# A routed-expert block whose gathers are reordered: tile loops written out, the lead of the down gathers raised from 16 to 24 rows, and gathers issued in turns of four up and four down rows

## The reference, cut to what matters

```python
def peer_block(xb, w_q, sub_keys, expert_u, expert_v):
    T = xb.shape[0]
    q = (xb @ w_q).reshape(T, PEER_HEADS, 2, PEER_HALF)
    s = jnp.einsum('thpd,hpkd->thpk', q, sub_keys)
    sv, si = lax.top_k(s, PEER_TOPK)
    cand = (sv[:, :, 0, :, None] + sv[:, :, 1, None, :]).reshape(T, PEER_HEADS, PEER_TOPK * PEER_TOPK)
    ...
    top_s, pos = lax.top_k(cand, PEER_TOPK)
    eidx = jnp.take_along_axis(cidx, pos, axis=-1)
    gate = jax.nn.softmax(top_s.astype(jnp.float32), axis=-1).astype(xb.dtype)
    u = jnp.take(expert_u, eidx, axis=0)
    act = jax.nn.gelu(jnp.einsum('thkd,td->thk', u, xb))
    v = jnp.take(expert_v, eidx, axis=0)
    return jnp.einsum('thk,thkd->td', gate * act, v)
```

## Time and profile before

| | |
|---|---|
| median of 3 runs | 4076.16 us (4074.84 to 4086.3) |
| profiled execution, its own time | 4073.35 us |
| its span | 4071.4 us |
| gathers of layer one, first to last | 523 to 2184 us |
| gathers of layer two, first to last | 2341 to 4002 us |
| bytes moved by gathers | 1073.87 MB of 1168.56 MB |

### The profile page before, as it was taken

The page is one execution under the profiler, slowest core; times in us unless marked ns, Lnnn a source line. Parts: engine busy times, 40 slices in busy tenths (PEclk is TensorE's granted clock), DMA queues, the critical chain, the costliest instruction groups (busy, mean ns, idle before and its releaser), DMA issues.

```text
span 4071.4 us, 34938 instructions
## 1 busy us (share of the span) xinstructions
PE 2006.1 (49%) x9949; PEld 931.6 (23%) x9949; DVE 2019.2 (50%) x4967; ACT 685.6 (17%) x1897; POOL 2056.6 (51%) x2098
## 2 busy tenths in 40 slices
PE   8998963443433333333437954333333333333447
PEld 3554541111111111111213431111111111111213
DVE  1425265555555555555552255555555555555551
ACT  2112121111111111112111111111111111112112
POOL 1413136565655555555562045555555555555661
PEclk9998886666666666666568976666666666666668
DMA  5312359898988888889997268888888888889992
GB/s 199 124 52 83 134 188 340 324 342 307 345 331 331 323 329 330 327 329 361 335 341 260 83 251 333 330 330 327 333 331 328 323 330 336 325 323 357 341 362 103
DMA packets 334241, 1168.56 MB, mean 287 GB/s; under 512 B 36026, under 2 KB 39380, under 8 KB 331732
## 3 DMA queue, kind: packets, MB, share of 16 engines
q0 software_dynamic: 294912, 1073.87, 70.2%
q1 hardware_dynamic: 39124, 92.27, 6.1%
HBM read 1163.92 MB, written 2.10 MB: 286 GB/s over the span
## 4 chain that ended last, share of the span: by engine, by line
another core or an unknown queue 47%; PE 18%; ACT 10%; issue 8%; DVE 6%; POOL 3%; DMA 3%; POOLq 0%; ACTq 0%; DVEq 0%
PE banks L701 14%; ACT ring L1405 4%; PE banks L1039 4%; DVE scr L1903 2%; ACT L1397 2%; ACT L1385 2%; POOL scr L646 2%; POOL ring L652 2%; DMA ring<-in_peer_up,idx_v 1%; DMA ring<-in_expert_v,idx_v 1%; ACT scr L1385 0%; ACT hT L1223 0%; ACT ring L1375 0%; ACT scr L1397 0%
## 5 line engine op out<-in xcount | busy, mean ns | idle before, releaser
L1039 PE MATMUL banks<-ring 128*32 128x512 f32 x4096 | 874.6, 950 | 1642.2 <-ACT ring L1405 736.6
L1903 DVE CUSTOM_DVE_ANT_0 scr<-scr,banks 128x1024 f32<-128x1024 f32 x1024 | 1207.2, 1218 | 578.7 <-DMA scr<-in_expert_u,idx 271.1
L646 POOL DMA_INDIRECT scr<-in_expert_u,idx x512 | 480.9, 939 | 542.4 <-DVE idx L1882 156.0
L646 POOL DMA_INDIRECT scr<-in_peer_down,idx x512 | 480.7, 939 | 422.9 <-DVE scr L1903 155.8
L1039 PEld LDWEIGHTS banks<-ring 128*32 128x32 f32 x4096 | 177.5, 153 | 2126.3 <-issue 1983.2
L652 POOL DMA_INDIRECT ring<-in_expert_v,idx_v x512 | 480.2, 938 | 312.7 <-issue 145.7
L652 POOL DMA_INDIRECT ring<-in_peer_up,idx_v x512 | 480.6, 939 | 306.5 <-issue 150.2
L701 PE MATMUL banks<-ring,scr 128*128 128x128 f32 (+1 forms) x2112 | 287.4, 297 | 8.6 <-ACT ring L1427 5.2
L701 PEld LDWEIGHTS banks<-ring,scr 128*128 128x128 f32 x2112 | 259.7, 201 | 85.0 <-issue 81.6
L1375 ACT ACTIVATE ring<-banks 128x256 f32<-128x256 f32 x64 | 24.5, 383 | 1457.6 <-remote 1391.4
L701 PE MATMUL banks<-ring,hT 128*128 128x512 f32 x512 | 224.6, 596 | 1.8 <-DVE hT L1808 1.0
(11 more groups left out here) (211 smaller groups left out, 2067.6 us busy)
## 6 DMA issues: line engine op xcount, KB each, us to landing
ring<-in_w_mod SPq DMA_DIRECT2D x12, 2048.0 KB, 8.8
ring<-in_w_in SPq DMA_DIRECT2D x7, 2048.0 KB, 12.9
scr<-in_peer_w_q SPq DMA_DIRECT2D x1, 8192.0 KB
scr<-in_peer_down,idx POOLq DMA_INDIRECT x512
ring<-in_peer_up,idx_v POOLq DMA_INDIRECT x512
scr<-in_w_q SPq DMA_DIRECT2D x1, 8192.0 KB
scr<-in_expert_u,idx POOLq DMA_INDIRECT x512
ring<-in_expert_v,idx_v POOLq DMA_INDIRECT x512
```

The lines of the kernel that those rows point to most:

```text
L646: nc.gpsimd.indirect_dma_start(u_rows[:, k % SLOTS, :], None, table_u, bass.IndirectOffsetOnAxis(idx[:, h % IDX_SLOTS, k:k + 1], 0)).then_ ...
L1039: last = nc.tensor.matmul(psum[2 + c][32 * g:32 * g + 32, :], spread[:, h % 2, k, :], v_rows[k % SLOTS][:, c * CW:(c + 1) * CW], start=(h ...
L1903: V.tensor_tensor_reduce(u_rows[:, k % SLOTS, :], u_rows[:, k % SLOTS, :], xn, 1.0, 0.0, ALU.mult, ALU.add, dots[:, h % 2, k:k + 1]).then_ ...
```

## The change

The tile loops and `hold` go, and all four engines run through `for j in range(32)` written out, with plain waits on constants. On POOL 24 down gathers come first (`U_LEAD`), then four up gathers, four down gathers that are 24 ranks ahead, four up gathers, and so on. On DVE the order becomes: route j + 1, weights j - 1, dot products 0 to 7 of j, softmax j + 1, dot products 8 to 15, pack_idx j + 1; `add_output` moves behind the ninth dot product of the next tile's second head. On PE `scores_q` j + 3 moves ahead of b0 of head j, `scores_s` j + 3 ahead of b1, `block_rows` ahead of b2 of a tile's seventh head, `move_weights` j + 1 ahead of b3 of head j, and `move_idx` j + 3 (instead of n + 2) to the end of head j. On ACT the order becomes gelu j, exponentials j + 2, copy of the weights and spread j, copies of head j + 3. Two gate tiles of the second layer's end get other banks, and TensorE waits there for `w_packed` once more.

```diff
 V_CREDIT = 64
+N_HEADS = TT * PH
+U_LEAD = TOPK + SLOTS
...
-        def move_bank(h, last_tile):
-            return 6 if last_tile and h == PH - 1 else 4 + h % 2
...
-        def hold(eng, s, value):
-            eng.wait_ge(s, value)
-            eng.sem_inc(passed, 1)
...
             def gathers(layer, table_u, table_v, last_projection):
-                def u_gather(n, h, k):
-                    hold(pool, u_used, n * TOPK + (k + 1))
+                n0 = layer * N_HEADS
...
+                def u_gather(j, k):
+                    n = n0 + j
+                    if k == 0:
+                        pool.wait_ge(routed, n + 3)
+                    pool.wait_ge(u_used, n * TOPK + (k + 1))
                     nc.gpsimd.indirect_dma_start(u_rows[:, k % SLOTS, :], None, table_u,
...
-                def v_gather(n, h, k):
-                    hold(pool, v_used, n * TOPK + (k + 1 - SLOTS + V_CREDIT))
+                def v_gather(j, k):
+                    n = n0 + j
+                    if k == 0:
+                        pool.wait_ge(idx_packed, n + 1)
+                    pool.wait_ge(v_used, n * TOPK + (k + 1 - SLOTS + V_CREDIT))
...
-                def token_block(first, more):
-                    for h in range(PH):
-                        u_too = h < PH - 1 or more
-                        hold(pool, idx_packed, first + (h + 1))
-                        if u_too:
-                            hold(pool, routed, first + (h + 4))
...
-                            if u_too:
-                                u_gather(first + (h + 1), (h + 1) % PH, k)
-                            v_gather(first + h, h, k)
-                n0 = layer * TT * PH
-                pool.wait_ge(routed, n0 + 3)
-                for k in range(TOPK):
-                    u_gather(n0, 0, k)
+                for i in range(U_LEAD):
+                    u_gather(i // TOPK, i % TOPK)
                 full(pool, *last_projection)
-                with pool.Fori(0, TT - 1) as b:
-                    token_block(b * PH + n0, True)
-                token_block(n0 + (TT - 1) * PH, False)
+                for first in range(0, N_HEADS * TOPK, QUADS):
+                    for i in range(first, first + QUADS):
+                        v_gather(i // TOPK, i % TOPK)
+                    for i in range(first + U_LEAD, min(first + U_LEAD + QUADS, N_HEADS * TOPK)):
+                        u_gather(i // TOPK, i % TOPK)
...
+                def scores_q(j):
+                    n, h = n0 + j, j % PH
+                    if h == 0 and j > 0:
...
-                    if not first:
+                    if j >= 2:
                         pe.wait_ge(s_copied, n - 1)
                         pe.wait_ge(idx_packed, n - 1)
...
-                def move_idx(n, h):
+                def move_idx(j):
+                    n = n0 + j
                     pe.wait_ge(idx_expanded, n + 1)
-                    to_quads(psum[4 + h % 2], 0, idx_x).then_inc(idx_moved, 1)
...
-                def move_weights(n, h, bank, more):
...
+                def move_weights(j):
+                    n = n0 + j
                     pe.wait_ge(weighted, n + 1)
+                    pe.wait_ge(s_copied, min(n + 3, n0 + N_HEADS))
                     pe.wait_ge(idx_packed, n + 1)
-                    if more:
-                        pe.wait_ge(s_copied, n + 3)
-                    to_quads(psum[bank], 2 * P, weight[:, h % 2, :, :]).then_inc(w_moved, 1)
...
-                def add_up(n, h, scores_too):
+                    to_quads(psum[4 + n % 2], 2 * P, weight[:, n % 2, :, :]).then_inc(w_moved, 1)
+                def add_up(j):
+                    n, h = n0 + j, j % PH
+                    if h == 0:
+                        pe.wait_ge(x_added, n // PH + 1)
+                    if j + 3 < N_HEADS:
+                        scores_q(j + 3)
                     for b in range(TOPK // QUADS):
-                        if b == 2 and scores_too:
-                            scores_q(n + 3, (h + 3) % PH)
-                        if b == 3 and scores_too:
-                            scores_s(n + 3, (h + 3) % PH)
+                        if b == 1 and j + 3 < N_HEADS:
+                            scores_s(j + 3)
+                        if b == 2 and h == PH - 2 and j + 2 < N_HEADS:
+                            pe.wait_ge(u_used, (n + 2) * TOPK + SLOTS)
+                            block_rows()
+                        if b == 3 and j + 1 < N_HEADS:
+                            move_weights(j + 1)
                         pe.wait_ge(spread_set, n * TOPK + QUADS * (b + 1))
...
-                def token_block(it, more, beside={}):
-                    for h in range(PH):
-                        if h == PH - 3 and more:
-                            pe.wait_ge(x_cur_set, it + 2)
-                        if h == 0:
...
-                            pe.wait_ge(u_used, it * (PH * TOPK) + (PH * TOPK + SLOTS))
-                            block_rows()
-                        if not more and h == PH - 1:
-                            all_empty(pe, *last_rows)
-                        move_weights(it * PH + h, h, move_bank(h, not more), h < PH - 2 or more)
-                        add_up(it * PH + h, h, h < PH - 3 or more)
-                        if h < PH - 2 or more:
...
+                    if j + 3 < N_HEADS:
+                        move_idx(j + 3)
...
-                def activations_and_weights(n, h, bank, beside=None):
+                def gelu_of(j):
+                    n = n0 + j
                     act.wait_ge(u_used, n * TOPK + (TOPK + SLOTS))
-                    nc.scalar.activation(gelu[:, h % 2, :], dots[:, h % 2, :], gelu_func).then_inc(gelu_done, 1)
-                    if beside:
-                        beside()
-                    hold(act, w_moved, n + 1)
-                    nc.scalar.activation(packed_w[:, h % 2, :], psum[bank][:, 2 * P:2 * P + TOPK], ACT.Copy).then_inc(w_packed, 1)
+                    nc.scalar.activation(gelu[:, n % 2, :], dots[:, n % 2, :], gelu_func).then_inc(gelu_done, 1)
...
+                def spread_out(j):
+                    n = n0 + j
+                    act.wait_ge(w_moved, n + 1)
+                    nc.scalar.activation(packed_w[:, n % 2, :], psum[4 + n % 2][:, 2 * P:2 * P + TOPK], ACT.Copy).then_inc(w_packed, 1)
                     act.wait_ge(w_packed, n + 1)
                     act.wait_ge(v_used, n * TOPK + (V_CREDIT - TOPK))
                     for k in range(TOPK):
...
-                def token_block(it, b, more, beside={}):
-                    for h in range(1, PH):
-                        head(it * PH + h, h, 3 if more else PH - 1 - h, beside.get(h), not more)
...
-                        head(it * PH + PH, 0)
+                        nc.scalar.activation(spread[:, n % 2, k, :], e32, ACT.Copy,
+                                             scale=packed_w[:, n % 2, col_of(k):col_of(k) + 1]).then_inc(spread_set, 1)
+                def head(j):
+                    gelu_of(j)
+                    if j - (TT - 1) * PH in beside:
+                        beside[j - (TT - 1) * PH]()
+                    if j + 2 < N_HEADS:
+                        softmax_exp(j + 2)
+                    spread_out(j)
+                    if j + 3 < N_HEADS:
+                        scores_out(j + 3)
+                    if j % PH == PH - 4 and j + PH < N_HEADS:
+                        rows_of(j // PH + 1)
...
-                def head(n, h, more=True, blocks=None, beside=None):
+                    V.tensor_tensor(X[:, t, :], peer_sum, X[:, t, :], ALU.add).then_inc(x_added, 1)
+                def head(j):
+                    more = j + 1 < N_HEADS
                     if more:
-                        route(n + 1, (h + 1) % PH)
-                    if h == 0:
-                        hold(dve, xn_ready, blocks)
-                    dot_products(n, h)
+                        route(j + 1)
+                    weights(j - 1)
+                    if j % PH == 0:
+                        dve.wait_ge(xn_ready, (n0 + j) // PH + 1)
+                    dot_products(j, range(SLOTS))
                     if more:
-                        softmax(n + 1, (h + 1) % PH)
-                    weights(n, h)
+                        softmax(j + 1)
+                    dot_products(j, range(SLOTS, SLOTS + 1))
+                    if j % PH == 1 and j > PH:
+                        add_output(j // PH - 1)
+                    dot_products(j, range(SLOTS + 1, TOPK))
                     if more:
-                        pack_idx(n + 1, (h + 1) % PH)
-                    if beside:
-                        beside()
...
-                with dve.Fori(0, TT - 1) as b:
-                    token_block(b + layer * TT, b, True)
-                token_block(TT - 1 + layer * TT, TT - 1, False, beside)
+                dot_products(0, range(SLOTS, TOPK))
+                softmax(1)
+                pack_idx(1)
+                for j in range(1, N_HEADS):
+                    head(j)
```

(57 more changed lines are left out.)

128 lines of the change are left out of this document (56 added, 72 removed).

## The result

The changed kernel takes 3791.44 us (median of 4 runs, 3781.11 to 3796.19) against 4076.45 before on the same chip: a ratio of 0.9302 [0.9281, 0.9322]. The forecast was 3915, in 3660 to 4120. The direction and the range held, but the gain is 285 us and not 161.

What follows compares the result with a forecast made beforehand. Neither an engine nor DMA alone bounds it: POOL's issue, 39.8 us a head, plus 11.4 of stalls. From 4073.35, 56 heads x 3.2 = 179 off and 20 on give 3914, as median 3915; range 3660 to 4120.

Steps and rivals of the forecast that it cites:

- stall B: POOL's wait before down gathers during DVE's pause between heads, 7 to 8 us a head; its cause would go.
- B's threshold of 16.3 us: DVE's pause between two heads' dot products costs POOL nothing up to 16.3 us; the new pause would be 10 to 15.5.
- Stall A's rule: POOL's up-gather wait, about 4.1 us: signals given 4 to 5 us or more into unbroken gathers are heard 3 us after.
- Two pauses a head: POOL's head: 39.8 us of issue plus two pauses of 4.1, 48.0 against 51.2, gaining 3.2 us; chance 0.45.
- Loops written out: Removing the tile loops and hold gets nothing: at most 0.3 us for each of 48 looped heads, 14 us.
- Boundaries and ends, +20: Late output-addition signals at 3 tile boundaries in 2 layers cost 0 to 42 us, taken as 20; start and end 0.
- One pause a head (2): Rival: one pause or less on POOL, 43.9 us a head, 7.3 less, 3664 us; chance 0.20.
- Rival 4: Slower: q's word heard only after the row, b1 to b3 a row later, third pause, 52.1 us a head; chance 0.15.
- Rival 3: No late words at all, DMA the only bound: 41 us a head, 3502 us; chance 0.10.

Runs made afterwards that it cites:

- e10: e1's kernel with 16 repeats of one 0.69 us instruction in each route, lengthening DVE's pause: 4712.17 us, 1.1372 of the kernel before, on a late chip.
- e12: The kernel before with its tile loops written out and hold's increments kept: 4044.79 us, ratio 0.9769, on a late chip.
- e1: The kernel before with its four tile loops written out and hold's increment left out, orders unchanged: 3506.81 us, ratio 0.9902, on a prompt chip.
- e11: The changed kernel with 8 repeats of one instruction in each route: 3862.09 us, 0.9312 of the kernel before, on a late chip.
- e5: The changed kernel as it is, on a prompt chip: 3512.16 us, 0.9922 of the kernel before.
- e6: The changed kernel with 20 down gathers ahead instead of 24: 3596.74 us, 1.0158 of the kernel before, on a prompt chip.
- e2: e1's kernel with POOL's program alone taken from the changed kernel, other engines in old orders: 4022.03 us, 1.1355 of the kernel before.
- e9: The kernel before as it is, run again for its trace, on a late chip: 4124.34 us in one run, against 4150.27.
- e8: The changed kernel with v_used and spread_set raised once a block by four, 24 fewer signals a head: 3511.27 us, 0.9918 of the kernel before.

## Why the prediction was right, and where it was not

**The bound and stall B: right.** Two stalls of POOL a head, B made by DVE's pause and A by late signals. B's threshold of 16.3 us was measured at about 16 in five traces, e10 lengthened pause and stall together, the new pause is 10.2, and B went.

**Stall A's rule: half right.** The prediction named rows of more than 20 gathers and signals heard within rows as signs that it is wrong, and both came. That a signal given more than 4 to 5 us into a row waits for its end holds for b3's (heard 10.6 us later) and for the weights' (16.6), but b2's, given 13 us into the row, was heard within it. What decides between them is not shown. So the forecast was right in its direction by B, and that its time lies 124 us off and yet in the range is in part luck.

**Two pauses a head: near in number (2.3), mis-sized.** The term 2 x 4.1 = 8.2 measured 6.3 (4.4 and 2.1 in the head shown), so the head is 46.2 and not 48.0. What failed is the step "Eight slots give at most eight up gathers, with eight down gathers between them, in one row": the rows are mostly 24 and 8 gathers, not 16 and 16, because signals of b1 and b2 are heard in the row's middle; and "Nothing shorter than 3 us after a row has been seen" held for rows of 15 and 17, while after a row of 8 it takes 2.1. The bounds of 6 to 8.4 us that the prediction kept did hold it.

**Loops written out, "This gets nothing": wrong.** e12 puts the edit at 98 us or 2.3% on a late chip, e1 together with hold's increments at 33 to 34 on a prompt one. The prediction had 14 at most, by comparing the looped tiles of one trace with its written-out fourth. That tile runs under other conditions: in e12 it is slower than three tiles of like form. The Trainium skill ("Runtime: NRT & Kernel Launch", section "Instruction fetch mechanics"), which speaks for unrolling, was on the right side here; the runs show the gain, and not that fetching of instructions makes it. How the 98 us enter the changed kernel's 285 wasn't split. In e12 they come by a shorter stall B, which the new orders remove anyway, so the two gains need not add. What separates e12's 0.977 from e11's 0.931 belongs to the orders and to hold, whose increments were not tried alone on a late chip.

**Boundaries and ends, +20: not there.** 56 x (51.2 - 46.2) = 280, and the profiled executions differ by 4073.35 - 3792.03 = 281. The 24 heads of each window hold three boundaries, so their cost is in these means. The signal of `add_output` is heard at once: it ends at 3011.50 (row below), and PE, idle for 0.88 us, starts at 3011.56. On a prompt chip, where POOL comes sooner, the same wait keeps PE idle for 10.2 us in each tile (e5).

```profile
3010.28 1.22 DVE L1911 TENSOR_TENSOR X<-banks,X 128x1024 f32<-128x1024 f32 x1 [0.76 <-remote]
```

**The rivals.** One pause a head (2) did not come. Rival 4 (whose sum makes 4143, not 4145) came in its first half: q's word was heard only after the row of 8, 5.03 us after its matmuls, and b1 came in the next row, so only four up gathers fit in the row of 8. The third pause did not follow, because the words of b1 and b2 let the next row run to 24. Rival 3, no late signals and DMA as the bound, gave 3502 and is nearly what a prompt chip shows, 3512, but there the kernel before takes 3541. The Trainium skill ("DMA: Bandwidth & Descriptors", section "Where 436 GB/s comes from") has about 358 GB/s as the limit that memory sets a core; e5 moved 406 GB/s over 1003 us with one core at work, so for this kernel that limit does not hold, and the measurement decides.

What the prediction could not know from one trace is that the late signals are not there on every chip. Its 7% is a gain where they are late.

## What to carry to other kernels

A long wait whose end the trace can only put down to "remote" is a hint that signals come late: look at the distance from the signalling instruction's end to the waiter's start, and time the kernel on another chip before tuning against it. Where one engine works between two parts of a ring of slots, its pause is free up to the slots' cover; measure that threshold, as pause less stall, and order the work so that the pause stays under it; a new order can move the threshold, as e11 shows. Work done once a tile can still cost more than the step in every head, as the output's addition does in e6. A new issue order and the orders of the engines that feed it are one change: the first of them without the others cost 13.6% here, on a prompt chip (e2).

## What the runs showed of the hardware

On the late chips, three of six if the first part's chip is one of its own, signals between engines arrive late while GpSimd issues indirect DMAs back to back. GpSimd itself goes on mostly 2.0 to 2.3 us after a row of 8 gathers has ended and 3.6 to 4.6 us after most rows of 17 to 25. A signal was heard up to 19.5 us after it was given in the heads shown (e9: q's matmuls end at 3020.62, ACT's copy starts at 3040.11), but some are heard in the middle of a row. On the other three chips no trace (e1 to e8) has a wait released by "remote" in its steady heads. The transfers are no slower (413 GB/s over 14 us on the first chip, 406 steady on a prompt one). The kernel before takes 4076 to 4150 us with late signals and 3541 without. Why they are late, whether the chip or something else on it at the time decides, and whether fewer signals would help there, stays open.
